# A hybrid MLA, SSD and mLSTM step on one core: mLSTM heads written out, scores and memory products in halves, output product begun early

## What is computed

```python
xm, o_pre, z, gates = jnp.split(h @ w_in, [ML_INNER, 2 * ML_INNER, 3 * ML_INNER], axis=-1)
xc = jax.nn.silu(centred_dwconv(xm, conv_w, conv_b))
q = jnp.einsum('blhd,hde->blhe', xc.reshape(b, n, ML_HEADS, ML_DH), w_q)
k = jnp.einsum('blhd,hde->blhe', xc.reshape(b, n, ML_HEADS, ML_DH), w_k) * (ML_DH ** -0.5)
v = jnp.einsum('blhd,hde->blhe', xm.reshape(b, n, ML_HEADS, ML_DH), w_v)
...
s = jnp.einsum('bihk,bjhk->bhij', qc, kc) * wmat
num = (jnp.einsum('bhij,bjhv->bihv', s, vc).astype(F32)
       + g_inter.swapaxes(1, 2)[..., None] * jnp.einsum('bihk,bhkv->bihv', qc, cs).astype(F32))
den = jnp.sum(s, axis=-1).astype(F32) + g_inter * jnp.einsum('bihk,bhk->bhi', qc, ns).astype(F32)
...
c_new = decay[..., None, None] * cs.astype(F32) + jnp.einsum('bhj,bjhk,bjhv->bhkv', w_end, kc, vc).astype(F32)
...
hh = (h_f + flip(h_b)) * jax.nn.sigmoid(o_pre).reshape(b, n, ML_HEADS, ML_DH)
hh = headwise_layernorm(hh, norm_g).reshape(b, n, ML_INNER)
out = ((hh + skip * xc) * jax.nn.silu(z)) @ w_out
```

## Time and profile before

| What | Value |
|---|---|
| Median of three runs | 3039.27 us |
| The profiled execution's own time | 3046.02 us |
| Its span, first to last instruction | 3044.5 us |
| Mean granted TensorE clock | 0.927 of full |
| TensorE busy | 2669.3 us (88%) |
| VectorE, ScalarE, GpSimd busy | 1226.7, 903.8, 1366.7 us |
| Chain that ended last: TensorE's share | 70% |

### The profile page before, as it was taken

One profiled execution on the slowest core, in us unless ns is written; L12 is line 12 of the kernel. 1 busy time (PEld: TensorE's weight loads), 2 busy tenths in 40 slices (PEclk: granted clock), 3 DMA queues, 4 the chain that ended last, 5 costly groups with the idle time before them and its releaser, 6 DMA issues.

```text
span 3044.5 us, 40444 instructions
## 1 busy us (share of the span) xinstructions
PE 2669.3 (88%) x16415; PEld 2218.3 (73%) x16415; DVE 1226.7 (40%) x1782; ACT 903.8 (30%) x1719; POOL 1366.7 (45%) x819
## 2 busy tenths in 40 slices
PE   7999988887788878696799899899899598999987
PEld 6976658877777777596784694695695398977667
DVE  3255552555655555513322412412422313165552
ACT  2144431433444444302221231221231201144431
POOL 2534445345654545450540641651651444545442
PEclk8999999988899888796899999999999798999998
DMA  7342203243444342231120220221221222221101
GB/s 239 101 127 73 77 24 98 72 134 105 139 118 119 103 114 61 85 96 38 43 78 28 71 83 23 84 70 37 70 74 47 89 67 84 70 72 21 29 17 60
DMA packets 293169, 238.94 MB, mean 78 GB/s; under 512 B 60878, under 2 KB 276496, under 8 KB 291972
## 3 DMA queue, kind: packets, MB, share of 16 engines
q1 hardware_dynamic: 285584, 200.38, 22.2%
q10 hardware_dynamic: 2404, 21.22, 1.7%
q0 software_dynamic: 5008, 14.81, 1.5%
HBM read 212.28 MB, written 24.09 MB: 78 GB/s over the span
## 4 chain that ended last, share of the span: by engine, by line
PE 70%; DVE 13%; ACT 6%; POOL 5%; issue 4%; POOLq 1%; DMA 1%; ACTq 0%; DVEq 0%; SPq 0%
PE ps L252 11%; PE ps L255 10%; PE ps L256 10%; PE ps L2362 4%; PE ps L1179 3%; PE ps L1243 3%; PE ps L2373 2%; PE ps L2306 2%; PE ps L1225 2%; PE ps L1574 2%; DVE room L1879 2%; POOL w_hi L271 2%; PE ps L2322 2%; PE ps L1577 2%; PE ps L1578 2%
## 5 line engine op out<-in xcount | busy, mean ns | idle before, releaser
L271 POOL TENSOR_TENSOR w_hi<-ring,ones 128x1024 fp32r<-128x1024 f32 (+1 forms) x190 | 382.9, 2015 | 627.4 <-DMA ring<-in_ssd_w_in_dram 166.2
L272 POOL TENSOR_TENSOR w_lo<-ring,w_hi 128x1024 fp32r<-128x1024 f32 (+1 forms) x190 | 476.7, 2509 | 14.9
L252 PE MATMUL ps<-h_hi,w_hi 128*128 128x320 f32 x992 | 319.4, 322 | 36.7 <-POOL w_lo L272 20.1
L252 PE MATMUL ps<-room_r,w_hi 128*128 128x320 f32 x960 | 304.0, 317 | 37.2 <-DVE room_r L739 28.4
L255 PE MATMUL ps<-h_lo,w_hi 128*128 128x320 f32 x992 | 315.2, 318 | 0.0
L256 PE MATMUL ps<-h_hi,w_lo 128*128 128x320 f32 x992 | 314.8, 317 | 0.0
L255 PE MATMUL ps<-room_r,w_hi 128*128 128x320 f32 x960 | 299.5, 312 | 0.0
L256 PE MATMUL ps<-room_r,w_lo 128*128 128x320 f32 x960 | 299.3, 312 | 0.0
L1388 POOL TENSOR_TENSOR room<-room 128x640 f32<-128x640 f32 (+1 forms) x148 | 164.8, 1151 | 243.5 <-DVE room L1328 243.5
L1574 PE MATMUL ps<-h_hi,w_hi 128*128 128x320 f32 x736 | 251.8, 342 | 2.7 <-POOL w_lo L272 2.7
L1577 PE MATMUL ps<-h_lo,w_hi 128*128 128x320 f32 x736 | 241.2, 328 | 0.0
(11 more groups left out here) (357 smaller groups left out, 5484.8 us busy)
## 6 DMA issues: line engine op xcount, KB each, us to landing
yT<-in_ada_w_dram SPq DMA_DIRECT2D x28, 1024.0 KB, 7.9
ring<-in_ssd_w_in_dram SPq DMA_DIRECT2D x48, 512.0 KB, 4.9
ring<-in_ml_w_in_dram SPq DMA_DIRECT2D x48, 512.0 KB, 4.6
room<-acs_rows SPq DMA_DIRECT2D x80, 256.0 KB, 5.2
ring<-in_mla_w_in_dram SPq DMA_DIRECT2D x24, 512.0 KB, 4.9
hT<-in_ada_w_dram SPq DMA_DIRECT2D x12, 1024.0 KB, 5.0
xT<-x_rows ACTq DMA_DIRECT2D x4, 2560.0 KB, 9.6
room<-in_ada_w_dram SPq DMA_DIRECT2D x8, 1024.0 KB, 12.5
```

Source lines behind the costliest of these rows:

```text
L252: mm = pe.matmul(wide(b)[:, c], hi, x_hi[:, c], start=start, stop=False)
L271: pool_t.after(pool.tensor_tensor(hi, raw, one.broadcast_to(raw.shape), ALU.mult))
L272: pool.tensor_tensor(lo, raw, hi.bitcast(F32), ALU.subtract).then_inc(w_split, 1)
```

## The change

Only layer 2 and its output product change.

- The loop over the heads is written out in the program on all engines.
- The order of a head's tiles is xm, v, z, q, k, o; the second half of o comes behind the first two numerators. The end of a head (turning keys, sums of n, state tiles, turning h) is put between the next head's four xm tiles and its first v tile (`tail_pe`).
- Scores and memory products use halves: ScalarE writes the high halves of q and k, VectorE the low ones; both slabs of the old memory are split by GpSimd; n is split once. All sums and products with n come in one piece, into one PSUM bank, and the denominators are made once a head.
- The gate products become plain f32 from a small array of their own and alternate with the first two xm tiles of head 0; scans and exponentials run beside the tiles that follow. The meeting of all engines behind the gates goes.
- The product with y moves from GpSimd to VectorE, the adding of the two directions into VectorE's numerators; GpSimd only gates h.
- The meeting behind the last head goes. The high halves of y are written during the last head, and 24 steps of the output product's first two tiles stand between the pieces of its end.

```diff
             else:
                 act.wait_ge(y_split, y_before(l - 1) + (KD if (l - 1) % 3 == 0 else KI))
+                if (l - 1) % 3 == 2:
+                    act.wait_ge(S["m_c_stored"], STORED * ML_HEADS)
...
-        kinds = ["xm"] * 4 + ["o"] * 2 * NT + ["z"] * 4 + ["q"] * 4 + ["k"] * 4 + ["v"] * NT
+        kinds = ["xm"] * 4 + ["v"] * NT + ["z"] * 4 + ["q"] * 4 + ["k"] * 4 + ["o"] * 2 * NT
...
+            pe.wait_ge(S["m_gates_loaded"], 16)
+            for k in range(KD):
+                pe.wait_ge(h_ready, KD * 2 + k + 1)
+                for tt in range(NT):
...
+                    pe.matmul(dst, h_hi[:, k, c].bitcast(F32), gate_w[:, k], start=(k == 0 and tt == 0), stop=False)
+                    mm = pe.matmul(dst, h_lo[:, k, c].bitcast(F32), gate_w[:, k], start=False, stop=(k == KD - 1 and tt == NT - 1))
...
+                for n in range(2):
+                    mm = split3_tile(pe, big((n + 1) % 2), hi[:, k, n * P:(n + 1) * P], lo[:, k, n * P:(n + 1) * P],
+                                     h_hi[:, k], h_lo[:, k], start=(k == 0), stop=(k == KD - 1))
...
+            fill[0]()
+            pe.wait_ge(S["m_i_read"], 9 * h + 8)
+            for k in range(KH):
+                mm = pe.transpose(bank(7)[:, k * P:(k + 1) * P], k_ctx[k], ident[:])
+            mm.then_inc(S["m_kt_done"], 1)
+            fill[1]()
+            pe.wait_ge(S["m_kw_ready"], h + 1)
+            pe.wait_ge(S["m_i_read"], 9 * h + 9)
+            for d in range(2):
+                mm = pe.matmul(bank(4 + d)[0:1, :], ones[:, 0:1], m_kw[:, d], start=True, stop=True)
+            mm.then_inc(S["m_n_done"], 1)
+            c_tile(0)
+            c_tile(1)
+            pe.wait_ge(S["m_n_copied"], h + 1)
+            c_tile(2)
+            c_tile(3)
+            fill[2]()
+            for n in range(4, 8):
+                c_tile(n)
+            fill[3]()
+            pe.wait_ge(S["m_ln_ready"], h + 1)
...
+            tail_h_turned(pe, h, 0)
+            tail_h_turned(pe, h, 1)
+            fill[4]()
+            tail_h_turned(pe, h, 2)
+            tail_h_turned(pe, h, 3)
...
                     for k in range(KH):
-                        mm = pe.matmul(bank(4 + j % 2)[:, 0:n], m_k[:, k, j * P:(j + 1) * P],
-                                       m_q[:, k, 0:LAT] if j < LC else m_q[:, k, LAT:TOK],
-                                       start=(k == 0), stop=(k == KH - 1))
+                        mm = split3(pe, dst, k_hi[:, k, c], k_lo[:, k, c], qh[:, k], ql[:, k],
+                                    start=(k == 0), stop=(k == KH - 1))
...
+                tile(h, "o", 0)
+                scores(h)
+                for i in range(1, NT):
+                    tile(h, "o", i)
+                sums(h)
+                inits(h, 0)
+                inits(h, 1)
+                num(h, 0)
+                num(h, 1)
+                for i in range(NT, 2 * NT):
+                    tile(h, "o", i)
+                for i in range(2, NT):
+                    num(h, i)
+            half = Y_EARLY // 2
+            tail_pe(pe, ML_HEADS - 1, [lambda m=m, c=c: ml_out_first(pe, [(m, n) for n in range(c * half, c * half + half)])
+                                       for m in range(2) for c in range(2)] + [lambda: None])
...
+                ins.then_inc(S["m_a_ready"], 1)
+                dve.wait_ge(S["m_a_ready"], KH * h + m + 1)
+                if m == 0:
+                    dve.wait_ge(S["m_rd_a"], act_read(h, "z", 3))
+                for s, c in ((0, slice(0, LAT)), (1, slice(C_CTX, CONV))):
+                    y = yT[:, KH * h + m, seg(s)]
+                    ins = dve.tensor_tensor(y, y, m_xc[:, m, c], ALU.mult)
+                ins.then_inc(S["m_y_ready"], 1)
...
+                for _ in range(3):
+                    split_slab(pool)
+
+                dmas = FIRST_DMAS if h == ML_HEADS - 1 else (HALVES, HALVES)
+                split_slab(pool, dmas[0])
+                for i in range(LC):
+                    h_part(h, i)
+                slot, _, full, _ = slabs.take(dmas[1])
+                split_half(pool, slot, full, 0)
+                h_part(h, LC)
+                split_half(pool, slot, full, 1)
+            stores(ML_HEADS - 1)
```

More of the change, by code:

```diff
@@ L2155, in ml_sync, with take, w_in @@
-            slabs.leave(ML_HEADS)
-        def ml_in_pe(pe):
+            n0 = t["state_mlstm_c"][0, 0]
+            def take(dst_n, src, kt, dmas=HALVES):
+                slot, free, _, _ = slabs.take(dmas)
+                sp.wait_ge(w_used, free)
+                dst = columns(ring, slot, dst_n)
+                if dmas is WHOLE:
+                    sp.dma_start(dst, src).then_inc(w_loaded[slot][0], 16)
+                else:
+                    load_halves(sp, slot, dst, src, kt)
+            def w_in(c, h, half):
+                at = INNER * c + DH * h + 2 * P * half
+                take(2 * P, w[:, :, at:at + 2 * P], KD)
@@ new lines, in hybrid_flow_step, with ml_out_sync @@
+        FIRST_DMAS = [tuple(len(FIRST_OUT[2 * n + h]) for h in range(2)) for n in range(2)]
+        def ml_out_sync(sp):
+            w = t["ml_w_out"][0].rearrange("(k p) n -> p k n", p=P)
+            for n in range(2):
+                slot, free, _, _ = slabs.take(FIRST_DMAS[n])
+                sp.wait_ge(w_used, free)
+                dst = columns(ring, slot, P)
+                for h in range(2):
+                    at = 8 * h
+                    for m, k0, k1 in FIRST_OUT[2 * n + h]:
+                        sp.dma_start(dst[:, at:at + k1 - k0], w[:, k0:k1, m * P:(m + 1) * P]
+                                     ).then_inc(w_loaded[slot][h], 16)
+                        at += k1 - k0
@@ new lines, in hybrid_flow_step, with ml_out_pe @@
+        ml_out_first.slab = None
+        def ml_out_pe(pe):
+            ml_out_first(pe, [(m, n) for n in range(Y_EARLY, KI) for m in range(2)])
+            for m in range(2, KD):
+                slot, _, _, split = slabs.take(HALVES)
+                hi, lo = columns(w_hi, slot, P), columns(w_lo, slot, P)
+                pe.wait_ge(out_read, KD * 2 + m + 1)
+                for k in range(KI):
+                    if k % (KI // 2) == 0:
+                        pe.wait_ge(w_split, split[k // (KI // 2)])
+                    mm = split3_tile(pe, big(m % 2), hi[:, k], lo[:, k], y3_hi[k], yT_r[:, k], start=(k == 0), stop=(k == KI - 1))
+                slab_through(pe, mm, last_cols(m % 2), out_done)
+                if m == 2:
+                    norm_sum(pe, 3, 0)
+                norm_sum(pe, 3, m - 1)
+            norm_sum(pe, 3, KD - 1)
```

1043 lines of the change are left out of this document (618 added, 425 removed).

## The result

| | before | after |
|---|---|---|
| Median, same chip | 3039.48 us | 2924.66 us (2922.74 to 2927.32) |
| Ratio | | 0.962 (0.960 to 0.964) |
| The profiled execution's own time | 3046.02 us | 2922.74 us |
| Its span | 3044.5 us | 2921.0 us |
| Mean granted clock | 0.927 | 0.930 |

The change saves 3.8%. Forecast were 2899 us, so the time lies 26 us above the forecast and inside the range. The spans differ by 123.5 us, and 123.3 of them lie in the stretch from the first gate product to the last output product: 1156.1 us before, 1032.8 after. So nothing outside moved between these two executions.

What follows compares the result with a forecast made beforehand. TensorE was taken to bound the layer. 21.9 + 5.7 + 831 + 21 + 5 + 8 + 123.2 = 1015.8 us instead of 1156.1, −140, gave 2906 profiled, 2899 us as median; range 2865 to 2947 us.

Steps and rivals of the forecast that it cites:

- the conversion: From profiled execution to median: the profiled one lies 6.7 us above the median shown, so 2906 becomes 2899 us.
- Work of a head: A head at full clock: 216.0 us, less 8.3 by scores and memory products in halves, so 207.7 us, 831 for four.
- The seam: Between one head's end and the next head's tiles: waits end within a tile; 1.2 us a head left, 5 in all.
- The sums gathered: Short products of a head in one 7.9 us piece: the clock falls, costing 5.3 us a head, 21 in all.
- Rival (b): Clock stays low through the start (+24 us) and the whole of each gathered piece (+17): 2940 us, chance 0.14.
- my own case: The forecast itself for the whole kernel, 2899 us, chance 0.56.
- The start: Gate stretch: 67.6 to 27.6 us, with 80 gate products at 17.9 us, +4 for half clock, 5.7 for transposes.
- The end: Last head's end before the output product: 5 us idle and 3 us of lower clock; output product 123.2 us.
- rival (c): VectorE is late at the next head, slowed beside GpSimd: 12 us a head, 2947 us, chance 0.12.
- (a): Short products hold the clock, in gathered sums and at the layer's start: without 21 and 4 us, 2874 us, chance 0.08.
- (d): Waits between heads come back among the new tiles, the end still waits for y: 76 us less gain, 2975 us, chance 0.06.
- (e): GpSimd's order makes each slab's load and split serial, from 35 us a head: 3045 us and more, chance 0.04.

Runs made afterwards that it cites:

- plain products: The changed kernel with scores and memory products as single f32 products of the high halves, the low halves' part left out: 2944.3 us, ratio 0.9678.
- warm start: The changed kernel with 15 unread f32 filler products of 256 columns in TensorE's waits of the norm before layer 2: 2916.95 us, ratio 0.9586.
- mixed start: The changed kernel with each gate product alone behind one dense product of 320 columns: 2942.11 us, ratio 0.9672; with filler ahead 2916.51 us, ratio 0.9590.

## Why the prediction was right, and where it was off

**The sum against the trace.** The stretch was forecast at 1015.8 us and took 1032.8, 17.0 more:

| Step | Forecast | Measured | Off |
|---|---|---|---|
| Start with xm 0 and 1 | 21.9 + 14.2 = 36.1 | 42.9 | +6.8 |
| Rest of the first head | 193.3 | 193.8 | +0.5 |
| Three periods | 3 × 214.2 | 645.1 | +2.5 |
| Last head's end and output product | 143.6 | 151.0 | +7.4 |

Here 193.3 is 207.7 without the end (12.4) and without the two xm tiles (14.2), with 5.7 for transposes, 5.3 for the clock and 1.2 of waits. The other 8.7 us of the miss are the conversion: I took the profiled execution before as 6.7 us above its median, and it was, but the one after lies 1.9 us below its own.

**Work of a head.** Right. The scores came to 12.5 us (27.18 for scores and five o tiles, 14.7 of them o's), forecast 14.9 − 2.5 = 12.4. Memory products: 0.235 us against 0.230. The plain products showed the gain by themselves. But that the three periods look right to 0.8 us each is in part luck: the clock cost 3.2 us more a head than forecast, the waits 1.2 less, and the work at full clock, 215.0 − 8.5 = 206.5 us, 1.2 less than the 207.7 worked out.

**The seam.** Right, and more so than said: no wait at all in place of 1.2 us a head, and 10.5 us a head come back when it is undone. Of the 14.6 us of waits that the kernel before had in a head, that kernel shows 9; the other part went with the changed splits and reads.

**The sums gathered.** The mechanism was right, since the granted clock falls in each head within the sums, as the earlier trace rows had suggested. The size was too small: I let half the piece double and took 1.7 us behind it, 5.3 us in all; measured were 7.0 us in the first head and 8.5 in the others. The clock falls earlier in the piece than I let it (2.5 us into a piece of 7.9 us, in three heads), and it lasts 5.7 us past the sums, over 13 memory products. Rival (b), with the whole piece at half rate and 9.6 us a head, was nearer here than my own case. (Half of the piece would have been 3.95 us, not the 3.6 of the sum; that changes 1.4 us in all.) What the step didn't see is that this was avoidable at no cost: single short products between dense ones give all of it back, 8.3 us a head.

**The start.** This step failed. "At half clock until the first dense piece": the first dense piece came after 4 us and lasted 3.5, and the clock stayed at 0.50 for 23.3 us, through three such pieces. It cost 10.9 us (the warm start's 32.0 against 42.9) where I had 4. In the other traces of the same start it cost 4.0 to 10.9 us, so the step describes the one execution in eight in which the clock rose after 8.4 us, and no more. At full clock the 80 products were priced well, 32.0 − 14.2 = 17.8 us against 17.9. Rival (b) had the right kind of mechanism here, at less than half its price. (By its own terms, 17.9 us and 96 products at 0.267 instead of 0.147, low clock throughout is 29.4 us and not 28; the mixed start measured 60.0 − 31.9 = 28.1.)

**The end.** 5 us of waits and 3 of clock were forecast; 8.0 us of idle time and 17.0 us at half clock, so 8.5 lost, came. The step that failed is the price of VectorE's operations, and with it the waits and the clock that follow them. I took 0.74 us for a low half and set nothing for GpSimd beside them, though the earlier trace rows show 0.89 us growing to 3.04 beside it and rival (c) was built on that. The six low halves took 12.8 us instead of 4.4. Reordering them won 8.7 us in the trace.

**Rival (c) at the seams.** VectorE's last low half of x ended at 1717.1 us, and q began at 1722.9: 5.8 us were left of the slack that I had put at 9. Two of the eight low-half operations before it show the stretch; GpSimd's split ran beside the first for 2.34 us and beside the second not at all:

```profile
1706.05 2.88 DVE L2789 TENSOR_TENSOR room_r<-room,room_r 128x512 fp32r<-128x512 f32 x1
...
1709.06 0.68 DVE L2789 TENSOR_TENSOR room_r<-room,room_r 128x512 fp32r<-128x512 f32 x1
```

So VectorE is stretched here too, which costs nothing at this place. It costs in the last head's end. The Trainium skill ("SBUF — State Buffer", section "SBUF: two separate sides") describes such a lock between the two engines; the trace agrees, with 0.68 us for the operation alone and 2.88 us beside the split.

**The other rivals.** (a) is refuted in the trace, clock 0.52 for 14 us at busy share 1. (d) is, by the seams without waits, and (e), since TensorE never waited for GpSimd in the stretch. The Trainium skill ("TensorE: Matmul & The Clock Gate", section "The HAM clock gate") says that activity releases the throttle and that it is set by how busy the engine was. Read as plain busy time, the traces contradict it: at busy share 1 both levels occur, side by side, with the same instructions. What else than busy time it answers to, no run here settles.

## What to carry to other kernels

When TensorE is busy all the time, read the granted clock next, by windows of a few microseconds: here some 52 us of one execution lay in it (10.9 at the start, 32 in the heads, 8.5 in the end) that no wait showed. Look at it in more than one execution: the same code lost 4 to 10.9 us at the start. Don't gather products of a few columns; drop them singly between dense ones, and see that TensorE enters such a mixture at full clock. Price each VectorE operation by the slowest of its kind in the trace where GpSimd works beside it, above all in an end that VectorE sets.

## What the hardware showed beyond that

- One mixture of short and dense products kept the clock that it found, low or high: one 16-column product to one of 320 columns ran 60.0 us at 0.50, and 31.9 us at 1.00 with filler ahead of it, in one trace each.
- Pieces of 1.9 us of short products, 3 to 4 us apart, still brought falls, on the dense products behind them (0.61 and 0.68 granted over two o tiles). The same products one or two at a time brought none in four heads.
- Fifteen filler products of 256 columns, placed where TensorE would have waited for VectorE and ScalarE anyway, repaid 10 us against the changed kernel's trace; the products behind them began 0.9 us later.
- What stays open: why the start of the changed kernel climbs after 8, 16 or 23 us with the same instructions, while the even mixture didn't in 60, and which mixtures lower a high clock. Only two were tried.
